# Loading x and one weight chunk first, and normalising the output by token as it leaves PSUM

## The reference

```python
def swiglu(x, w_in, w_out):
    g, u = jnp.split(x @ w_in, 2, axis=-1)
    return (jax.nn.silu(g) * u) @ w_out
# every layer
x = x + 0.5 * swiglu(rmsnorm(x, norm_ffn1), w_ffn1_in, w_ffn1_out)
...
x = x + 0.5 * swiglu(rmsnorm(x, norm_ffn2), w_ffn2_in, w_ffn2_out)
# at the end
y = x * rsqrt(mean(x * x, axis=-1) + EPS) * norm_final
```

## Time and profile before

| | us |
|---|---|
| median of 3 runs | 2075.08 |
| the profiled execution's own time | 2073.86 |
| its span in the profile | 2071.7 |
| TensorE busy | 1878.4 (91%) |
| VectorE busy | 1297.4 (63%) |
| ScalarE busy | 835.2 (40%) |
| GpSimd busy | 212.9 (10%) |
| mean granted TensorE clock | 0.951 of full speed |

### The profile page before, as it was taken

The page is one execution under the profiler, slowest core; times in us unless marked ns, Lnnn a source line. Parts: engine busy times, 40 slices in busy tenths (PEclk is TensorE's granted clock), DMA queues, the critical chain, the costliest instruction groups (busy, mean ns, idle before and its releaser), DMA issues.

```text
span 2071.7 us, 34322 instructions
## 1 busy us (share of the span) xinstructions
PE 1878.4 (91%) x13481; PEld 1676.7 (81%) x13481; DVE 1297.4 (63%) x2322; ACT 835.2 (40%) x1104; POOL 212.9 (10%) x305
## 2 busy tenths in 40 slices
PE   6999895898988689899999999999998798999996
PEld 5999895887865345698769999999986697689996
DVE  4665486587885655457537665766656677266654
ACT  4433354244655543333224334433444542144332
POOL 0001100200110001021111001000311021110011
PEclk9999998899998889898999999999999998999998
DMA  6666843234793468576526656665744476536652
GB/s 181 180 167 174 177 152 119 92 100 135 220 295 126 137 215 285 187 251 235 206 92 175 180 164 198 177 180 158 218 136 131 144 243 246 203 93 175 180 166 77
DMA packets 463035, 360.93 MB, mean 174 GB/s; under 512 B 14601, under 2 KB 435749, under 8 KB 462885
## 3 DMA queue, kind: packets, MB, share of 16 engines
q1 hardware_dynamic: 409056, 253.82, 41.7%
q0 software_dynamic: 20320, 71.95, 11.1%
q10 hardware_dynamic: 33552, 33.70, 4.8%
HBM read 320.96 MB, written 38.66 MB: 174 GB/s over the span
## 4 chain that ended last, share of the span: by engine, by line
PE 74%; DVE 10%; ACT 8%; issue 5%; DMA 2%; SPq 0%; ACTq 0%; POOL 0%; DVEq 0%; POOLq 0%
PE psum L255 18%; PE psum L256 18%; PE psum L257 18%; PE psum L2004 3%; ACT whi L208 2%; PE psum L1550 2%; DVE wlo L214 2%; PE psum L605 2%; DMA raw<-in_w_in_ab 1%; PE psum L466 1%; PE psum L754 1%; PE psum L235 1%; PE psum L250 1%; PE psum L236 1%; PE psum L237 1%
## 5 line engine op out<-in xcount | busy, mean ns | idle before, releaser
L214 DVE TENSOR_TENSOR wlo<-raw,whi 128x2048 fp32r<-128x2048 f32 (+2 forms) x262 | 557.4, 2128 | 286.4 <-ACT whi L208 285.8
L255 PE MATMUL psum<-xnh,whi 128*128 128x264 f32 x2328 | 678.0, 291 | 9.6 <-DVE cols L930 7.9
L256 PE MATMUL psum<-xnl,whi 128*128 128x264 f32 x2328 | 667.3, 287 | 0.0
L257 PE MATMUL psum<-xnh,wlo 128*128 128x264 f32 x2328 | 666.4, 286 | 0.0
L208 ACT ACTIVATE whi<-raw 128x2048 fp32r<-128x2048 f32 (+2 forms) x262 | 462.7, 1767 | 154.7 <-DMA raw<-in_w_ffn_out 77.5
L255 PEld LDWEIGHTS psum<-xnh,whi 128*128 128x128 f32 x2328 | 446.7, 192 | 34.1 <-issue 23.2
L256 PEld LDWEIGHTS psum<-xnl,whi 128*128 128x128 f32 x2328 | 447.0, 192 | 0.2
L257 PEld LDWEIGHTS psum<-xnh,wlo 128*128 128x128 f32 x2328 | 444.3, 191 | 0.0
L255 PE MATMUL psum<-Hh,whi 128*128 128x264 f32 x704 | 200.5, 285 | 0.0
L257 PE MATMUL psum<-Hh,wlo 128*128 128x264 f32 x704 | 200.0, 284 | 0.0
L256 PE MATMUL psum<-Hl,whi 128*128 128x264 f32 x704 | 199.1, 283 | 0.0
(11 more groups left out here) (510 smaller groups left out, 3068.6 us busy)
## 6 DMA issues: line engine op xcount, KB each, us to landing
raw<-in_w_ffn_in SPq DMA_DIRECT2D x176, 512.0 KB, 4.9
raw<-in_w_in_ab SPq DMA_DIRECT2D x88, 512.0 KB, 4.5
raw<-in_w_ffn_out SPq DMA_DIRECT2D x64, 384.0 KB, 4.0
raw<-in_w_ffn_out SPq DMA_DIRECT2D x64, 320.0 KB, 3.4
sb<-in_state_ret POOLq DMA_DIRECT2D x32, 512.0 KB, 5.0
out<-sb ACTq DMA_DIRECT2D x32, 512.0 KB, 3.9
raw<-in_w_out_ab SPq DMA_DIRECT2D x32, 512.0 KB, 4.9
kc<-in_cache_mem_k POOLq DMA_DIRECT2D x32, 512.0 KB, 5.8
```

The costliest lines, as they stand in the source:

```text
L214: nc.vector.tensor_tensor(wlo[:, c % SLOTS, 0:m], raw[:, c % SLOTS, 0:m], whi[:, c % SLOTS, 0:m].bitcast(F32), ALU.subtract).then_inc(lo_d ...
L255: e.matmul(out, a, hi[:, kk, 0:S.cols], start=first, stop=False)
L256: e.matmul(out, a, lo[:, kk, 0:S.cols], start=False, stop=False)
L257: m = e.matmul(out, b, hi[:, kk, 0:S.cols], start=False, stop=final)
```

## The change

Three parts. In the head, SyncE holds back the load of chunk 1, and all behind it, until x has landed, and GpSimd does the same with `rot`, `dtab` and `tail`; `FirstSplit` is cut in two, so that chunk 1 is split behind `SplitX`; `Select` moves to the start of the first mixer; and the first norm's squares are summed on GpSimd (`FirstSquares`), so that `XStat` takes the place of `Stat`. In the last `residual`, ScalarE scales each finished tile by its gain into `yT`, and TensorE transposes it (`TurnY`) two chunks later into banks 4 to 7, 1 and 3. After it, `LastNorm` makes the mean square with the tokens on the partitions, and `Final` scales by token on the way out of PSUM and stores in five pieces.

```diff
             def sp(S, e):
                 def load(i, r):
                     slot = (S.c0 + r) % SLOTS
+                    if S.c0 + r == 1 and isinstance(i, int):
+                        e.wait_ge(x_in, 32)
...
-                walk(e, S.n, load)
+                walk(e, S.n, load, first=2 if S.c0 == 0 else 0)
...
             def act(e, l, par, use):
+                if final:
+                    e.wait_ge(bank_free, use + 3)
+                    final(l)
                 if gcol is None:
                     return
...
                 e.dma_start(p2[96:120, :], A["ssd_conv_b"].rearrange("l (t p) -> (l t) p", p=P)).then_inc(p_in, 16)
+                e.wait_ge(x_in, 32)
                 e.dma_start(rot[:, :, :], A["c_rot"]).then_inc(consts, 16)
...
         class FirstSplit(Stage):
 
+            def __init__(S, r):
+                S.r = r
+
             def act(S, e):
-                for r in range(LEAD):
-                    linears[0].split_hi(e, 0, r)
+                linears[0].split_hi(e, 0, S.r)
 
             def dve(S, e):
-                for r in range(LEAD):
-                    linears[0].split_lo(e, 0, r)
-        stages.append(FirstSplit())
+                linears[0].split_lo(e, 0, S.r)
+
+        class FirstSquares(Stage):
...
+            def pool(S, e):
+                e.memset(acc[:, :, :], 0.0).then_inc(acc_done, 1)
+                x_ready(e)
+                for l in range(4):
+                    e.wait_ge(acc_done, S.a0 + l + 1)
+                    xs = x[:, 2 * l:2 * l + 2, :]
+                    e.tensor_tensor(sq[:, :, :], xs, xs, ALU.mult).then_inc(xs_ready, 1)
+                    e.wait_ge(xs_ready, S.q0 + l + 1)
+                    e.tensor_tensor(acc[:, :, :], acc[:, :, :], sq[:, :, :], ALU.add).then_inc(acc_done, 1)
+        stages.append(FirstSplit(0))
+        FirstSquares()
...
             def pe(S, e):
                 e.wait_ge(sel_done, 1)
-        stages.append(Select())
...
             residual(w_out, 2 * KD, KF // 2, 1, by_rows(w_out, KF // 2), (Hh, Hl), 0.5, gcol,
-                     ready=at_least(h_ready, f0 + KF // 2 + 2), cpu=2, hooks={0: [HReady()]}, by_token=True)
+                     ready=at_least(h_ready, f0 + KF // 2 + 2), cpu=2, hooks={0: [HReady()], **turns}, by_token=True, final=final)
...
         def mixer_ab():
             W = A["w_in_ab"][0]
+            stages.append(Select())
...
         SplitX(G_FFN1, all_of(x_ready, gains_ready))
-
-        class RstdWait(Stage):
+        stages.append(FirstSplit(1))
...
+        y_bank = lambda part, half: (4 + half, 6 + half, 1 + 2 * half)[part]
+
+        def scale_y(t):
+            nc.scalar.activation(yT[:, t, :], x[:, t, :], ACT.Copy, scale=g1[:, G_FIN + t:G_FIN + t + 1]).then_inc(y_scaled, 1)
+
+        class TurnY(Stage):
...
+            def pe(S, e):
+                t, c = S.t, slice(S.t % 4 * P, (S.t % 4 + 1) * P)
+                e.wait_ge(y_scaled, t + 1)
+                for b in range(2):
+                    e.transpose(psum[:, y_bank(b, t // 4), c], yT[:, t, b * P:(b + 1) * P], ident[:, :])
+                e.transpose(psum[0:NS, y_bank(2, t // 4), c], yT[:, t, NP:T], ident[:, :]).then_inc(tp_done, 1)
+
+        class RootTable(Stage):
...
+            def act(S, e):
+                nc.scalar.activation(cols[:, 58:59], ones[:, 0:1], ACT.Sqrt)
+
+        class LastNorm(Stage):
...
+            def pe(S, e):
+                e.wait_ge(acc_done, S.acc)
+                for b, s in ((0, slice(0, P)), (1, slice(P, NP)), (2, slice(NP, T))):
+                    o = psum[0:s.stop - s.start, S.bank, b:b + 1]
+                    e.matmul(o, acc[:, 0, s], ones[:, 0:1], start=True, stop=False)
+                    m = e.matmul(o, acc[:, 1, s], ones[:, 0:1], start=False, stop=True)
+                m.then_inc(xss_done, 1)
+
             def dve(S, e):
-                e.wait_ge(rstd_done, 1)
-
-        def first_stat():
-            Stat(x, 1, KD, rstd1)
-            stages.append(RstdWait())
+                e.wait_ge(xss_done, S.n)
+                e.tensor_scalar(rstdc[:, 0:2], psum[:, S.bank, 0:2], 1.0 / D, EPS, ALU.mult, ALU.add)
+                e.tensor_scalar(rstdc[0:NS, 2:3], psum[0:NS, S.bank, 2:3], 1.0 / D, EPS, ALU.mult, ALU.add).then_inc(y_scaled, 1)
+                e.wait_ge(xsd_done, S.n)
+                e.reciprocal(rstdc[:, 0:2], rstdc[:, 0:2])
+                e.reciprocal(rstdc[0:NS, 2:3], rstdc[0:NS, 2:3]).then_inc(xrs_done, 1)
+                e.wait_ge(xrs_done, S.n)
+
+            def act(S, e):
+                e.wait_ge(y_scaled, KD + 1)
+                nc.scalar.activation(rstdc[:, 0:2], rstdc[:, 0:2], ACT.Sqrt)
+                nc.scalar.activation(rstdc[0:NS, 2:3], rstdc[0:NS, 2:3], ACT.Sqrt).then_inc(xsd_done, 1)
+
+        class Final(Stage):
...
+            def act(S, e):
+                e.wait_ge(tp_done, S.t0 + KD)
+                e.wait_ge(xrs_done, S.n)
+                for half in range(2):
+                    nc.scalar.activation(ytok[:, 0, half * 512:(half + 1) * 512], psum[:, y_bank(0, half), :], ACT.Copy, scale=rstdc[:, 0:1]).then_inc(tpa, 1)
+                nc.scalar.activation(ystok[:, 0:512], psum[0:NS, y_bank(2, 0), :], ACT.Copy, scale=rstdc[0:NS, 2:3]).then_inc(tpa, 1)
+
+            def dve(S, e):
+                e.wait_ge(tp_done, S.t0 + KD)
+                for half in range(2):
+                    e.tensor_scalar(ytok[:, 1, half * 512:(half + 1) * 512], psum[:, y_bank(1, half), :], rstdc[:, 1:2], None, ALU.mult).then_inc(tpd, 1)
+                e.tensor_scalar(ystok[:, 512:1024], psum[0:NS, y_bank(2, 1), :], rstdc[0:NS, 2:3], None, ALU.mult).then_inc(tpd, 1)
+
+            def sp(S, e):
...
+                for half in range(2):
+                    c = slice(half * 512, (half + 1) * 512)
+                    e.wait_ge(tpa, a + half + 1)
+                    store(e, "sp", O[0][0, 0:P, c], ytok[:, 0, c])
+                    e.wait_ge(tpd, d + half + 1)
+                    store(e, "sp", O[0][0, P:NP, c], ytok[:, 1, c])
+                e.wait_ge(tpa, a + 3)
+                e.wait_ge(tpd, d + 3)
+                store(e, "sp", O[1].rearrange("b o d -> (b o) d"), ystok[:, :])
+
         for layer in range(2):
-            ffn(layer, A["w_ffn1_in"][layer], A["w_ffn1_out"][layer], G_MIX + 8 * layer, stat=first_stat if layer == 0 else None)
+            last = layer == 1
+            ffn(layer, A["w_ffn1_in"][layer], A["w_ffn1_out"][layer], G_MIX + 8 * layer)
             (mixer_ab if layer == 0 else mixer_c)()
             cross(layer)
-            ffn(layer, A["w_ffn2_in"][layer], A["w_ffn2_out"][layer], G_FFN1 + 8 if layer == 0 else None)
...
-        XStat()
-        Apply(x, 1, KD, rstd1, G_FIN, None, None, out=yT)
...
-        Turn(items, ready=lambda e: e.wait_ge(y_scaled, 1))
...
+            ffn(layer, A["w_ffn2_in"][layer], A["w_ffn2_out"][layer], None if last else G_FFN1 + 8, final=scale_y if last else None,
+                turns={2 * t + 3: [TurnY(t)] + ([RootTable()] if t == 5 else []) for t in range(KD - 1)} if last else {})
+        stages.append(TurnY(KD - 1))
+        LastNorm()
+        Final()
```

More of the change, by code:

```diff
@@ L354, in by_rows, with residual @@
             return parts
-        def residual(W, n, kt, tiles, parts, rhs, scale, gcol, ready=None, cpu=1, hooks=None, by_token=False, kwise=None):
+        def residual(W, n, kt, tiles, parts, rhs, scale, gcol, ready=None, cpu=1, hooks=None, by_token=False, kwise=None, final=None):
             q0, a0, u0, s0 = tot["xq"], tot["xacc"], tot["use"], tot["app"]
@@ L684, in build, with __init__ @@
         class FirstSplit(Stage):
+            def __init__(S, r):
+                S.r = r
             def act(S, e):
-                for r in range(LEAD):
-                    linears[0].split_hi(e, 0, r)
+                linears[0].split_hi(e, 0, S.r)
             def dve(S, e):
-                for r in range(LEAD):
-                    linears[0].split_lo(e, 0, r)
-        stages.append(FirstSplit())
+                linears[0].split_lo(e, 0, S.r)
+        class FirstSquares(Stage):
+            def __init__(S):
+                S.q0, S.a0 = tot["xq"], tot["xacc"]
+                tot["xq"] += 4
+                tot["xacc"] += 5
+                tot["nx"] += 1
+                stages.append(S)
+            def pool(S, e):
[9 more added lines that the diff above has]
+        FirstSquares()
         sel_done = sem_of("sel_done")
@@ L758, in build, with ffn @@
         Hl = place("Hl", [P, KF, T], F32R, at=H_at + KF * T * 4)
-        def ffn(layer, w_in, w_out, gcol, stat=None):
+        def ffn(layer, w_in, w_out, gcol, stat=None, final=None, turns={}):
             f0, q0 = tot["ffn"], tot["gate"]
@@ L2726, in build @@
         SplitX(G_FFN1, all_of(x_ready, gains_ready))
-        class RstdWait(Stage):
-            def dve(S, e):
-                e.wait_ge(rstd_done, 1)
-        def first_stat():
-            Stat(x, 1, KD, rstd1)
-            stages.append(RstdWait())
```

(50 more changed lines are left out.)

2 lines of the change are left out of this document (removed).

## The result

The changed kernel took **2062.84 us** (median of four runs, 2060.29 to 2064.2) beside 2076.51 (2074.56 to 2078.28) of the kernel before on the same chip: a ratio of 0.9935, 95% interval 0.9919 to 0.9951, 13.7 us faster. The forecast of 2057.4 was 5.4 too low; 2062.84 lies just inside the wide range of 2053 to 2063 and outside the forecast's own range of 2053.5 to 2060.5.

A forecast was written before the change was run, and what follows sets the result against it. TensorE multiplying weight chunks back to back bounds the kernel, so only the ends gain: head 7.1 + tail 12.1 - turns 2.7 = 16.5 us off 2073.86, giving 2057.4 (own range 2053.5 to 2060.5, wide range 2053 to 2063).

The forecast's parts named there:

- x and the load order: Head, loading: no gain taken for x; tables landing at about 15, with 18.4 as the late bound.
- the second rival: Head: tables land at 22 instead of 15, the gains wait, 4.1 us are lost: 2061.5; chance 0.08.
- so I add 0.3: Head, low split of chunk 0: GpSimd squaring beside it adds 0.3 us, first matmul at 20.05, 4.1 earlier.
- The sums, 3.6 saved: Head, first norm's sums: they hold TensorE 0.79 us in place of 4.37, saving 3.6.
- The third rival: Head: GpSimd blocks VectorE altogether during a pass, delaying chunk 0's low split 2.8 us, not 0.3: 2059.9; chance 0.04.
- Bank wait of chunk 2, 0.6: Head, behind chunk 0: the root comes late, so chunk 2 waits for its first free bank; 0.6 us lost.
- `Select`, 3.8 late and covered: First mixer: TensorE waits for `Select`, chunk 0 starts 3.8 us late, covered by the late fifth chunk with 2.7 to spare.
- The first rival: First mixer: `Select`'s stall isn't covered, as the fifth chunk is delayed equally: 2057.4 + 3.8 = 2061.2; chance 0.12.
- a sign of being wrong: First mixer: a fifth-chunk wait on TensorE still of 6.5 us, where 2.7 was expected, would make the forecast wrong.
- The turns, 2.7: Last block: six `TurnY` between chunks cost 0.45 us each, 2.7 lost, between 1.9 and 4.3.
- The fourth rival: Last block: turns break TensorE's run, matmuls behind each go at half rate, 47 us more: 2104; chance 0.03.
- The tail, end at 11.35 after the last result: Tail: span ends 11.35 us after the last matmul's result against 23.5, saving 12.1, between 10 and 13.

The follow-up runs named there:

- e3: The changed kernel with GpSimd's first squares and sums cut from 264 columns to 4 of each tile: 2059.3 us, ratio 0.9916 to the kernel before.
- e14: The same kernel as e3 (changed kernel, GpSimd's first squares and sums cut to 4 columns), profiled once more: 2058.86 us in one execution.
- e12: The kernel before, unedited, for one more profiled execution: 2079.2 us.
- e5: The changed kernel again, unedited, for more executions and a second trace: 2064.86 us, ratio 0.9947 to the kernel before.

## Why the prediction was wrong

By the medians the change gave 13.7 us where 16.5 were forecast: 2.8 of the 5.4 us. The other 2.6 are the base, the profiled execution of 2073.86 beside a median of 2076.51. The step that failed is GpSimd beside VectorE: 0.3 us were taken for it, and it cost the head most of the 2.6 us by which it fell short; with GpSimd's passes cut (e3) the head gained 8.1, 3.6 more.

- **x and the load order:** right, no gain taken, none measured; the tables were there at 16.31, and the second rival (22) was not it.
- **GpSimd beside the low split, "so I add 0.3":** this is the step that failed. Of the earlier trace rows I read only VectorE's side. GpSimd's timeline of the kernel before has the other:

```profile
2002.37 2.12 POOL L414 TENSOR_TENSOR acc<-acc,sq 128x264 f32<-128x264 f32 x1
...
2026.02 0.76 POOL L414 TENSOR_TENSOR acc<-acc,sq 128x264 f32<-128x264 f32 x1
```

  The second pass ended at 2026.78 and the subtraction began at 2026.36: only 0.42 us lay side by side, and 0.27 of it were added. That is again the time side by side less 0.15, so a full block and no rate. The first pass shows it outright: a sum of 0.75 us alone took 2.12 beside a subtraction that had begun 0.11 us before it (2002.26, 1.63 us). The third rival had the mechanism, and had 0.04 for it. It too looked at the low split alone, which lost 0.55, since it slipped in between two passes, and left out the eight low parts of x, which lost 4.6. First matmul at 21.16, not 20.05 (0.2 of it is x); chunk 0 then waits once more for a low part (0.46 us) and takes 8.34 us, not 7.39, the rest of that mostly by a longer stretch at the low clock; chunk 1 begins at 30.19, not 28.2. That is 2.0 us, of which x and the clock have some 0.7.
- **The sums, 3.6 saved:** held; they take 0.69.
- **Bank wait of chunk 2, 0.6:** measured 1.2, the same size as in the earlier trace rows. Here it comes from the GpSimd step too: VectorE, held up before, is busy with two late low splits from 27.53 to 32.01, and the root's first operation comes only at 31.93, though the sums are done by 30.2. In e3 and e14 there is no such wait. The head gave 4.5 us, not 7.1: 2.0 and 0.6 less.
- **`Select`, 3.8 late and covered:** the cover was right, its size wrong. The wait was 4.4 us. GpSimd took part of that too: its sum ran until 222.24 beside the selection matrix, which took 0.70 us instead of 0.15:

```profile
221.56 0.70 DVE L727 TENSOR_TENSOR sel<-ident 40x8 fp32r<-40x8 f32 x1
```

  The mixer's first matmul is at 222.32, before at 222.21. But the fifth chunk decides what comes after: its high split is at 251.69, before at 254.68, so split 42 stands 3.0 us earlier than before, and only 0.7 of the 3.7 gained up to split 38 are lost. The first rival would have lost 3.8. From these times TensorE's wait should have shrunk to 3.4 us (6.5 - 3.0 - 0.1); it stayed at 6.7, which the prediction had named as a sign of being wrong. TensorE did the work in between in 3.3 us less, and waited for the chunk all the same. Before, it had idled 1.9 us until 230.97, about when the state `crow`, whose load was issued at 226.36 and took 4.5 us, landed, and more of its matmuls had run at the low clock. Stretches of TensorE before and after:

```profile
234.00:240.00 6.00, 6.00 (x33) 6.00 (x32) 2.29 (x1) 2.15 (x3) 0.00 (x0) 0.58 0.15 22
```

```profile
222.00:228.00 6.00, 5.68 (x34) 5.68 (x35) 2.56 (x2) 2.16 (x2) 4.57 (x8) 0.72 1.45 83
...
234.00:240.00 6.00, 6.00 (x53) 6.00 (x51) 3.01 (x4) 3.32 (x5) 0.00 (x0) 1.00 1.37 1
```

  At 234 to 240 it makes 53 matmuls where it made 33.
- **The turns, 2.7:** three pairs of chunks took 8.32 for 8.02, so about 0.31 a turn and 1.9 us, the lower bound of 0.105 for a transpose. The fourth rival's half rate never came.
- **The tail, end at 11.35 after the last result:** 10.5; 13.0 saved instead of 12.1. The twelve small matmuls took 1.2 us, below both bounds, which I had taken from transposes of 128 columns.
- **The middle, taken as unchanged:** about 3.7 us were lost between splits 199 and 222 at a lower clock. No term stood for it, and e12 shows that the kernel before moves by such amounts too.

With the measured terms: 4.5 - 0.7 - 1.9 + 13.0 = 14.9, less 3.7 is 11.2; the medians' 13.7 and, for e5, 11.9 lie around that. That 2062.84 fell inside the wide range at all is partly luck: the turns and the tail came out 1.7 us better than forecast, against 2.6 lost in the head and 0.7 at the mixer.

## What to carry to other kernels

When a row gives the price of two engines side by side, divide by the time that they overlapped, look at the timeline of both, and apply the result to every instruction in reach, not only to the one that was looked at. A stall that costs nothing may only stand in front of another one; look for the cause of that one first: here two loads of 4 KB in 4-byte pieces cost 9.2 us up to split 42, more than the 4.5 that the whole new head gained. Terms under 5 us in a kernel of 2 ms need more than one profiled execution of it as a base.

## What the runs showed of the hardware that was not expected

GpSimd's passes and VectorE's two-input passes from SBUF keep each other out for all but 0.12 to 0.15 us of the time that they lie side by side: 0.20 us became 2.14, and 0.484 became a median of 1.292. Two loads of 4 KB in 4-byte elements took 18.4 us each, and 192 KB behind them landed after 23.4 us instead of 3.6. And the granted clock fell to 1.2 GHz in one kernel and stayed at 2.4 in another behind the same waits (0.65 and 1.00 in the same 3 us); in the table this comes as steps of 1 to 3 us.
